# Split products in the projection and the feed-forward: reordering the matmuls of a weight tile from chunk by chunk to block by block

## The reference

```
q, kc, vc, ks, vs, kw, vw, gn, u, v, ga, gb = split(rms_norm(x) @ w_in)      # 1024 x 4376 weight
o_a = native sparse attention(...);  o_b = gmlp_spatial(u, v)
x = x + (sigmoid(ga) * (o_a @ w_branch_a) + sigmoid(gb) * (o_b @ w_branch_b)) @ w_out
x = x + cross_attend(rms_norm(x), ...)
h = rms_norm(x)
x = x + (silu(h @ w_gate) * (h @ w_up)) @ w_down                             # hidden width 2816
y = rms_norm(x)
```

## Time and profile before

| | us |
|---|---|
| runs: median (lowest to highest of 3) | 2216.21 (2214.37 to 2217.53) |
| profiled execution: span | 2214.8 |
| TensorE busy (PE) | 2118.7 (96%) |
| weight loads busy (PEld, beside PE) | 1962.7 (89%) |
| DVE, ACT, POOL busy | 929.5, 551.1, 611.8 |

### The profile page before, as it was taken

How to read it: one execution, slowest core, us unless ns; L and a number is a source line. 1 busy time by engine, 2 the same in 40 slices (tenths; PEclk the granted TensorE clock), 3 DMA queues, 4 the chain that set the end, 5 groups by cost and what they waited for, 6 DMA issues and landing times. The chain is left out here.

```text
span 2214.8 us, 38450 instructions
## 1 busy us (share of the span) xinstructions
PE 2118.7 (96%) x14076; PEld 1962.7 (89%) x14076; DVE 929.5 (42%) x1958; ACT 551.1 (25%) x1151; POOL 611.8 (28%) x531
## 2 busy tenths in 40 slices
PE   7999999988989999799999988999999999999998
PEld 6999999965855767599999878999999999999997
DVE  4111111186336676455661346563333333333335
ACT  5002211122326655222030332221111111111112
POOL 2233322245224444412212322212212122121220
PEclk9999999999979999899999999999999999999999
DMA  6212222394323000544212432110211112111121
GB/s 199 55 47 62 72 90 93 127 262 151 90 62 136 1 2 1 142 146 146 85 39 67 191 120 62 46 49 29 67 31 55 48 33 62 33 53 48 33 62 78
DMA packets 206648, 175.77 MB, mean 79 GB/s; under 512 B 25867, under 2 KB 186348, under 8 KB 205963
## 3 DMA queue, kind: packets, MB, share of 16 engines
q1 hardware_dynamic: 197450, 152.96, 22.7%
q10 hardware_dynamic: 4448, 11.81, 1.5%
q0 software_dynamic: 4640, 9.61, 1.5%
HBM read 147.02 MB, written 27.39 MB: 79 GB/s over the span
## 5 line engine op out<-in xcount | busy, mean ns | idle before, releaser
L152 POOL TENSOR_TENSOR tail_w_lo<-mem_last_slot,tail_w_hi 128x1024 fp32r<-128x1024 f32 (+1 forms) x94 | 183.3, 1950 | 689.8 <-ACT tail_w_hi L140 689.8
L191 PE MATMUL ff_psum<-tail_hi,tail_w_hi 128*128 128x352 f32 x1056 | 341.2, 323 | 1.0 <-PEq L2112 1.0
L192 PE MATMUL ff_psum<-tail_lo,tail_w_hi 128*128 128x352 f32 x1056 | 338.5, 321 | 0.0
L193 PE MATMUL ff_psum<-tail_hi,tail_w_lo 128*128 128x352 f32 x1056 | 338.2, 320 | 0.0
L191 PE MATMUL bank<-mix_hi,in_w_hi 128*128 128x352 f32 x840 | 271.9, 324 | 1.3 <-issue 1.3
L192 PE MATMUL bank<-mix_lo,in_w_hi 128*128 128x352 f32 x840 | 270.0, 321 | 0.0
L193 PE MATMUL bank<-mix_hi,in_w_lo 128*128 128x352 f32 x840 | 269.9, 321 | 0.0
L140 ACT CAST tail_w_hi<-mem_last_slot 128x1024 fp32r<-128x1024 f32 (+1 forms) x94 | 81.2, 863 | 509.3 <-PE ff_psum L193 433.4
L191 PEld LDWEIGHTS ff_psum<-tail_hi,tail_w_hi 128*128 128x128 f32 x1056 | 198.1, 188 | 2.0 <-issue 1.5
L192 PEld LDWEIGHTS ff_psum<-tail_lo,tail_w_hi 128*128 128x128 f32 x1056 | 198.4, 188 | 0.1
L193 PEld LDWEIGHTS ff_psum<-tail_hi,tail_w_lo 128*128 128x128 f32 x1056 | 197.9, 187 | 0.0
(11 more groups left out here) (394 smaller groups left out, 3822.2 us busy)
## 6 DMA issues: line engine op xcount, KB each, us to landing
in_raw<-w_in SPq DMA_DIRECT2D x70, 256.0 KB, 3.2
mem_last_slot<-w_gate SPq DMA_DIRECT2D x44, 256.0 KB, 3.2
mem_last_slot<-w_up SPq DMA_DIRECT2D x44, 256.0 KB, 3.3
mem_last_slot<-w_down SPq DMA_DIRECT2D x80, 128.0 KB, 2.2
gate_kept<-x_first ACTq DMA_DIRECT2D x16, 528.0 KB, 2.7
uv<-gate_kept SPq DMA_DIRECT2D x16, 528.0 KB, 4.6
mem_ring<-cache_mem_v SPq DMA_DIRECT2D x8, 1024.0 KB, 13.2
mem_ring<-cache_mem_k SPq DMA_DIRECT2D x7, 1024.0 KB, 7.0
```

The costliest lines, as they stand in the source:

```text
L152: pool.tensor_tensor(lo, raw, hi.bitcast(F32), ALU.subtract).then_inc(self.split, 1)
L191: pe.matmul(out, hi, x_hi, start=k == 0, stop=False)
L192: pe.matmul(out, hi, x_lo, start=False, stop=False)
L193: last = pe.matmul(out, lo, x_hi, start=False, stop=k == len(terms) - 1)
```

## The change

A new method `multiply_tile_by_weight` takes a whole tile at once: it waits for `split` and for all three banks, then for each block k sends hi*hi for the three chunks, hi*lo for the three chunks and lo*hi for the three chunks, each chunk into its own bank. The three banks are finished by the tile's last three matmuls, each of which raises `done`. `multiply` gets an argument `by_weight` that says which of the two tiles of an iteration go this way.

It is used for all tiles of the projection's loop, for the gate tiles (not the up tiles) of the feed-forward's loops, and for down tiles 2 to 7 of each group. The first two down tiles of a group are taken out of the loop and keep chunk order and the wait for the hidden columns; the other six no longer have that wait. The number of matmuls, their operands and the other engines' programs stay as they are.

```diff
--- before.py
+++ after.py
@@ -206,6 +206,24 @@
             if after is not None:
                 after(c)
 
+    def multiply_tile_by_weight(self, pe, it, step, m, groups):
+
+        s = m % 2
+        pe.wait_ge(self.split, step * it + (m + 3))
+        pe.wait_ge(self.freed, 3 * step * it + (3 * m + CH))
+        chunks = [groups((3 * m + c) % self.sets, c)[0] for c in range(CH)]
+        depth = len(chunks[0][2])
+        for k in range(depth):
+            hi, lo = self.w_hi[s][:, k, :], self.w_lo[s][:, k, :]
+            for out, _, terms in chunks:
+                pe.matmul(out, hi, terms[k][0], start=k == 0, stop=False)
+            for out, _, terms in chunks:
+                pe.matmul(out, hi, terms[k][1], start=False, stop=False)
+            for out, _, terms in chunks:
+                last = pe.matmul(out, lo, terms[k][0], start=False, stop=k == depth - 1)
+                if k == depth - 1:
+                    last.then_inc(self.done, 1)
+
     def multiply_pair(self, pe, groups, by_k, after):
 
         for q in range(2 * CH):
@@ -215,10 +233,13 @@
             self.terms(pe, m, groups(q % self.sets, c), (by_k, KD * c) if m == 0 else None)
             after(q)
 
-    def multiply(self, pe, first, tiles, groups, ready=None):
+    def multiply(self, pe, first, tiles, groups, ready=None, by_weight=()):
         with pe.Fori(0, tiles // 2) as it:
             for s in range(2):
-                self.multiply_tile(pe, it, 2, first + s, groups, ready)
+                if s in by_weight:
+                    self.multiply_tile_by_weight(pe, it, 2, first + s, groups)
+                else:
+                    self.multiply_tile(pe, it, 2, first + s, groups, ready)
 
     def place_halves(self, sb, ctx, name, depth, slots=(0, 1)):
         for s in slots:
@@ -725,7 +746,7 @@
                     turn(t)
                 pe.wait_ge(gain_set, 1)
                 st.multiply_pair(pe, products(ps, hi, lo), split, between)
-                st.multiply(pe, 2, GN - 2, products(ps, hi, lo))
+                st.multiply(pe, 2, GN - 2, products(ps, hi, lo), by_weight=(0, 1))
                 st.multiply_tile(pe, 0, 0, GN, products(ps, hi, lo))
 
             def take_rows(eng, copy, h, t):
@@ -2300,11 +2321,14 @@
                     if f == 0:
                         st.multiply_tile(pe, 0, 0, up_at, groups, by_k=late.split)
                         st.multiply_tile(pe, 0, 0, up_at + 1, groups, after=lambda c: late.spread_sums(pe, sums) if c == 0 else None)
-                        st.multiply(pe, up_at + 2, 2 * size - 2, groups)
+                        st.multiply(pe, up_at + 2, 2 * size - 2, groups, by_weight=(0,))
                     else:
-                        st.multiply(pe, up_at, 2 * size, groups)
+                        st.multiply(pe, up_at, 2 * size, groups, by_weight=(0,))
                     if down_at < last_at:
-                        st.multiply(pe, down_at, KD, products(ps, a_hi, a_lo, size), (chain, 3, 9 * (f + size)))
+                        down = products(ps, a_hi, a_lo, size)
+                        for m in range(2):
+                            st.multiply_tile(pe, 0, 0, down_at + m, down, (chain, 3, 9 * (f + size)))
+                        st.multiply(pe, down_at + 2, KD - 2, down, by_weight=(0, 1))
 
                 def turn(t):
                     pe.wait_ge(st.freed, st.sets + last_q + KD * (1 if t < 4 else 2 if t < 7 else 3))
```

## The result

The kernel after takes 2232.52 us (median of 4 runs, 2232.38 to 2233.24), the kernel before on the same chip 2216.87 us (4 runs, 2214.37 to 2218.95): a ratio of 1.0063, interval 1.005 to 1.0076. So the change makes the kernel slower, by some 14 us by the ratio (11 to 17 by its interval; the two medians lie 15.7 us apart). The forecast was 2216.5 us, no difference that can be told, and 2232.5 lies 7.5 us above the range's upper end.

What follows compares the result with a forecast made beforehand. TensorE was taken as the bound: matmul count times step between starts. Late starts 1.5 + 0.2, down tiles -1.4 and 4896 x 0 gave +0.3 on the 2216.2 us median: 2216.5 us, range 2204 to 2225.

Steps and rivals of the forecast that it cites:

- Weight loads saved, 0: Reordered tiles: each matmul call still brings its own load, and a repeated block steps no faster; 0 loads saved.
- Banks, 0 ns: Reordered tiles: going to another bank at every matmul makes the step neither shorter nor longer, 0 ns per matmul.
- The upper end of the unknown, +1.34 ns: Reordered matmuls: the most the step was allowed to grow, taken from the down tiles' longer step.
- Down tiles, -1.4 us for fewer waits: Reordered down tiles: with fewer waits per matmul they take the other tiles' step, 158.98 ns, saving 1.4 us.
- The wait for three banks: Start of a reordered tile: all three banks must be free; 0 us in the steady loop, evictions being covered.
- The two starts: Projection's tile 2 and the second gate tile wait uncovered for a third eviction: +1.5 us and +0.2 us.
- Clock: TensorE at projection's tile 2: the clock should survive the idle time of the late start.
- C: Rival: the new order steps as the down tiles do, 160.32 ns everywhere; +6.8, 2223 us; chance 0.18.
- A: Rival: the new order removes the loss per matmul, 61.6 us less before the two starts; 2156 us; chance 0.14.
- B: Rival: the loss sits in waits at chunk starts, 32 ns per start; 5.3 us less, 2212.6 us; chance 0.17.
- D: Rival: each change of bank costs about 31 ns, paid at every reordered matmul; +150 us, 2366; chance 0.03.
- E: Rival: the clock falls in each of the 83 reordered tiles; +134 us, 2350; chance 0.02.

Runs made afterwards that it cites:

- e5_blocks: Kernel after with weight blocks in the new order, columns in the old order and the bank in runs of 24 (no product): 2219.37 us.
- e2_banks: Kernel after with blocks and columns back in chunk order, only the bank changed at every matmul (no product): 2220.23 us.
- e6_columns: Kernel after with columns in the new order, weight blocks in the old order and the bank in runs of 24 (no product): 2236.18 us.
- e1_frame: Kernel after with its one wait and three completions per tile kept, matmuls put back in chunk order: 2219.41 us, ratio 1.0003.
- e4_align: Kernel before with every large SBUF tile moved by 32 bytes: 2215.48 us, ratio 0.9987.
- e17_apart64: Kernel after with projection weights 64 bytes higher, even projection tiles reading only row 0, odd ones only row 1 (no product): 2225.32 us.
- e16_apart128: Kernel after with projection weights 128 bytes higher, even projection tiles reading only row 0, odd ones only row 1 (no product): 2224.72 us.
- e12_runs: Kernel after reading other columns (no product): projection row 1 only, or rows 0 and 1 in runs of six; gates in runs of three: 2219.23 us.
- e13_by_block: Kernel after still block by block in three banks, but with each chunk's three matmuls per block together; product computed: 2215.08 us.

## Why the prediction was wrong

- *What bounds the kernel*: right. The reordered stretches are matmuls times step before and after, TensorE at 100% and clock 1.00, and the other engines covered.
- *Which matmuls*: right, 768 x 3 in the projection by the page, and 4896 in all.
- *Weight loads saved, 0*: right. 14076 loads, and `e5_blocks` shows that a repeated block is worth nothing.
- *Banks, 0 ns*: right as far as banks go (`e2_banks`). **The step that failed is the next one: "So I take 0 ns per matmul" was used for the whole order, 4896 x 0.** The prediction went through banks, blocks and waits, and never asked how the columns follow each other, the third thing that the diff alters and the one that `e6_columns` shows to carry the whole loss per matmul: +2.87, +2.67 and +1.08 ns, 11.8 us. The rows of before held one hint: the same matmul has two steps, 158.98 and 160.32, and the column floor of 146.7 ns explains neither.
- *The upper end of the unknown, +1.34 ns*, was taken from the nearest row, the down tiles. It was too low by a factor of two in the projection and the gate tiles, because that row was put down to waits and bank changes and so looked like the worst case. That is why the range ended at 2225.
- *Down tiles, -1.4 us for fewer waits*: wrong. `e1_frame` takes the waits away and leaves 160.37; `e4_align` moves buffers, keeps the waits, and brings 159.06. In the kernel after the term has the other sign, +1.2 us.
- *The wait for three banks*: 0 us in the steady loop, right (`e1_frame`). The two starts came as worked out, 1.44 for 1.5 us and 0.19 for 0.2 us, the first with the releaser that was named (the DVE row behind the copy). The up tiles kept their order but not their step, which the prediction took as unchanged: 0.29 ns, 0.4 us in all.
- *Clock*: right, 1.00 in all three stretches and from 54.76 to 78.16 us, behind the 1.44 us of idle time.
- *Rivals.* C named the right way to fail, an order that gets a longer step with no row to predict it, at a chance of 0.18; its size, 160.32, fell short, for the reason above. A falls with `e2_banks` and `e5_blocks`, B with `e1_frame` (one waiting start a tile in place of three, the same 158.98), D with `e2_banks`, E with the clock.

What stays open is why one sequence of start addresses is dearer than another. It is shown that the columns' order is the cause of the loss, that moving the weights alone changes the step (`e17_apart64` against `e16_apart128`), and that the place of a tile in the run has a part in it (`e12_runs`); no law was found, neither from the columns' own addresses nor from their distance to the weights. That the column stream and the weight load beside it meet at the memory would fit, but is argued, not shown. The Trainium skill, "TensorE: Matmul & The Clock Gate", section "Step-by-step: what each phase is for", says that the two are read through ports of their own and that a load takes no bandwidth from the running matmul. By that rule the place of the weights would leave the step alone; these runs do not agree, with 160.0 ns for row 0 in `e17_apart64` and 158.3 in `e16_apart128`.

## What to carry to other kernels

When a loop is bound by TensorE at full clock, its time is the count times the step between starts, so compare counts in a fixed window, not busy shares, and ask of a new order three questions: which bank, which block, which columns follow each other. Here the first two were free and the third cost 1.8%, and keeping the uses of the same columns next to each other kept the old step in block order too (`e13_by_block`). That is what these addresses gave and not a rule: the same columns 72 times made 161.1 ns in row 0. Swapping one of the three at a time, with the others held, settles in two or three runs what no row of the profile before could say.

## What the runs showed that was not expected

- The same 128x128 by 352-column matmul with its own load, at clock 1.00, steps between 158.3 and 161.9 ns, by the addresses of its operands, the reads before it and the place of its tile in the run (158.9 or 159.9 ns for the same gate tile of `e12_runs`).
- Moving the weight buffers by another 64 bytes took 160.0 to 158.3 ns for the same reads (`e17_apart64`, `e16_apart128`).
- Moving the large buffers by 32 bytes, and so the down tiles' columns by 64 against their weights, took the down tiles from 160.4 to 159.1 ns and made the kernel before faster by 0.13% (interval 0.03 to 0.24).
